# ScalarE's order in the second attention, step sizes in four blocks, and the first unit's waits by feature

## The reference

```python
def second_block(x, w_in, conv_w, conv_b, dt_bias, a_log, ...):
    proj = jnp.einsum('bsd,de->bse', x, w_in[layer])
    q, k, v, z_att, z_ssm, xbc, dt_raw = jnp.split(proj, list(SPLITS), axis=-1)
    # three dilated windows over q, k, v (dilations 1, 4, 16), 16 heads of 64,
    # put together by the softmax of their log-sums
    xbc = jax.nn.silu(causal_depthwise_conv(xbc, conv_w[layer], conv_b[layer]))
    dt = jax.nn.softplus(dt_raw + dt_bias)          # 16 numbers per token
    # chunked state-space scan over xbc and dt, norms, out projection, residual, layer norm
```

## Time and profile before

| | us |
|---|---|
| Median of 3 runs | 1773.06 (1771.41 to 1774.6) |
| The profiled execution | 1772.61 |
| Its span in the trace | 1770.8 |
| TensorE busy | 1717.6 (97%) |
| VectorE busy | 1187.0 (67%) |
| GpSimd busy | 888.1 (50%) |
| ScalarE busy | 812.8 (46%) |

### The profile page before, as it was taken

The page is one execution under the profiler, slowest core; times in us unless marked ns, Lnnn a source line. Parts: engine busy times, 40 slices in busy tenths (PEclk is TensorE's granted clock), DMA queues, the critical chain, the costliest instruction groups (busy, mean ns, idle before and its releaser), DMA issues.

```text
span 1770.8 us, 30057 instructions
## 1 busy us (share of the span) xinstructions
PE 1717.6 (97%) x11616; PEld 893.3 (50%) x11794; DVE 1187.0 (67%) x2237; ACT 812.8 (46%) x1622; POOL 888.1 (50%) x805
## 2 busy tenths in 40 slices
PE   8999999999999999999999999999999999999998
PEld 5534455455444456544445455544455555555543
DVE  5768889999999688431445578967155555555647
ACT  4523554443312677412322378843255655555720
POOL 0511543662661223687810257979566555772750
PEclk9999999999999999999999999999999999999999
DMA  9010111202321112212411246512211112111512
GB/s 399 26 54 36 54 48 66 78 24 102 161 96 52 68 66 102 120 59 105 180 60 70 93 165 197 199 35 98 89 39 53 58 34 58 34 52 56 207 65 95
DMA packets 53373, 161.84 MB, mean 91 GB/s; under 512 B 7056, under 2 KB 21776, under 8 KB 49008
## 3 DMA queue, kind: packets, MB, share of 16 engines
q1 hardware_dynamic: 49008, 136.36, 21.6%
q0 software_dynamic: 4224, 23.56, 3.4%
HBM read 129.35 MB, written 27.39 MB: 89 GB/s over the span
## 4 chain that ended last, share of the span: by engine, by line
PE 67%; DVE 20%; POOL 3%; ACT 3%; issue 3%; DMA 2%; SPq 0%; DVEq 0%; ACTq 0%; POOLq 0%
PE ps L1411 29%; PE ps L1891 14%; DVE small L2670 6%; PE ps L1405 4%; DVE arena L2423 4%; PE ps L1751 2%; PE ps L1434 2%; PE ps L1475 2%; PE ps L1533 2%; PE ps L1910 2%; DMA hT<-in_mods 2%; PE ps L1683 1%; PE ps L1507 1%; PE ps L1448 1%; PE ps L1515 1%
## 5 line engine op out<-in xcount | busy, mean ns | idle before, releaser
L1411 PE MATMUL ps<-hT,W 128*128 128x512 bf16 x2359 | 529.2, 381 | 10.5 <-ACT arena L1994 3.4
L1411 PEld LDWEIGHTS ps<-hT,W 128*128 128x128 bf16 x2424 | 236.1, 98 | 291.6 <-issue 12.2
L989 POOL TENSOR_TENSOR W<-W 128x512 bf16<-128x512 f32 x133 | 155.1, 1202 | 259.8 <-DMA W<-in_loads 189.6
L1411 PE MATMUL ps<-W,arena 128*128 128x512 bf16 x918 | 207.0, 380 | 1.1
L2097 ACT ACTIVATE arena<-arena,small 128x128 f32<-128x128 f32 (+9 forms) x192 | 123.1, 642 | 139.1 <-DVE small L2500 119.7
L1411 PEld LDWEIGHTS ps<-W,arena 128*128 128x128 bf16 x936 | 91.2, 97 | 112.0
L2670 DVE TENSOR_SCALAR_CACHE_REDUCE small<-arena,small 128x640 bf16<-128x640 f32 (+1 forms) x124 | 126.5, 1077 | 1.1
L974 POOL TENSOR_TENSOR arena<-arena 128x512 f32<-128x512 f32 (+1 forms) x62 | 104.8, 1691 | 43.6 <-DMA arena<-gates_scratch 19.1
L1411 PE MATMUL ps<-arena,W 128*128 128x512 bf16 x569 | 124.6, 379 | 1.2 <-POOL arena L1050 0.6
L2106 ACT ACTIVATE arena<-arena,small 128x128 f32<-128x128 f32 (+9 forms) x192 | 113.9, 644 | 18.6 <-DVE small L2458 18.6
L1891 PE MATMUL ps<-arena,W 128*128 128x512 bf16 x475 | 109.6, 379 | 1.1 <-issue 0.3
(11 more groups left out here) (391 smaller groups left out, 3225.8 us busy)
## 6 DMA issues: line engine op xcount, KB each, us to landing
W<-in_loads SPq DMA_DIRECT2D x20, 2048.0 KB, 8.0
arena<-sums_scratch SPq DMA_DIRECT2D x30, 512.0 KB, 4.6
W<-in_groups SPq DMA_DIRECT2D x56, 256.0 KB, 3.9
W<-in_loads SPq DMA_DIRECT2D x5, 1792.0 KB, 7.2
gates_scratch<-arena SPq DMA_DIRECT2D x32, 256.0 KB, 2.0
arena<-gates_scratch POOLq DMA_DIRECT2D x2, 4096.0 KB, 13.3
W<-in_mods SPq DMA_DIRECT2D x2, 2048.0 KB, 17.0
hT<-in_mods SPq DMA_DIRECT2D x2, 2048.0 KB, 21.3
```

The costliest lines, as they stand in the source:

```text
L989: last = nc.gpsimd.tensor_tensor(low(v), v, high(v), ALU.subtract)
L1411: last = mm(o, left[:, :, a], moving, start=(k == 0 and (a, b) == PRODUCTS[0]), stop=(k == steps - 1 and (a, b) == PRODUCTS[-1]))
```

## The change

Three edits. The `dt` units no longer run 512 tokens through 16 columns of the array: each product is four matmuls of 128 tokens, and each of the four writes its own strip of 32 partitions of PSUM. ScalarE puts them side by side with four copies. The wait for all 16 low parts ahead of the third unit of `xbc0` becomes one wait for each feature block inside that unit. In the second attention ScalarE's order within an iteration becomes: exponents of n, scalings of n, high parts of n-1, reads of sums. The first attention keeps its order.

```diff
-                if name == "dt":
-                    return KD, [(full, lambda k: parts(dt_weights[:, k, :]), lambda k: acts(hT, k, half, 512))]
...
+                if name == "dt":
+                    for k in range(KD):
+                        left = parts(dt_weights[:, k, :])
+                        for a, b in PRODUCTS:
+                            for r in range(4):
+                                last = mm(ps[32 * r:32 * r + 16, unit_bank(u), 0:P], left[:, :, a],
+                                          h_parts(k, 512 * i + P * r, P)[:, :, b], start=(k == 0 and (a, b) == PRODUCTS[0]),
+                                          stop=(k == KD - 1 and (a, b) == PRODUCTS[-1]), skip_group_check=True)
+                    last.then_inc(s_unit, 1)
+                    return
...
+                        if (name, i) == ("xbc0", 1):
+                            pe.wait_ge(s_hlow, KD + KD + k + 1)
...
-            pe.wait_ge(s_hlow, KD + 16)
...
+                elif name == "dt" and i < 2:
+                    for r in range(4):
+                        last = A(dtT[0:16, 512 * i + P * r:512 * i + P * r + P], ps[32 * r:32 * r + 16, unit_bank(u), 0:P],
+                                 ACT.Copy)
...
                         A(t, t, ACT.Exp, bias=mneg4[...], scale=-1.0, accum_out=den[...]).then_inc(sems["exp"], 1)
-                    extra(n, 0)
-                    if n >= 1:
-                        high_parts(n - 1)
+                    if tiles is at1:
+                        extra(n, 0)
                     act.wait_ge(sems["inverse"], n + 1)
                     act.wait_ge(sems["exp"], 2 * n + 2)
                     for x in range(2):
                         A(t, t, ACT.Copy, scale=rden[...]).then_inc(sems["scaled"], 1)
+                    if tiles is at2:
+                        if n >= 1:
+                            high_parts(n - 1)
+                        extra(n, 0)
                     extra(n, 1)
                     value_parts(n)
```

More of the change, by code:

```diff
@@ L1388, in unit @@
                     return
-                rows_ = slice(0, 72 if name == "small" and i < 2 else 16 if name == "dt" else P)
+                if name == "dt":
[8 more added lines that the diff above has]
+                    return
+                rows_ = slice(0, 72 if name == "small" and i < 2 else P)
                 steps, pieces = operands(name, i)
@@ L2006, in evac @@
                     last = A(gate[:, 512 * r:512 * r + 512], bank, ACT.Copy)
+                elif name == "dt" and i < 2:
+                    for r in range(4):
+                        last = A(dtT[0:16, 512 * i + P * r:512 * i + P * r + P], ps[32 * r:32 * r + 16, unit_bank(u), 0:P],
+                                 ACT.Copy)
                 elif name == "dt":
-                    last = A(dtT[0:16, half], bank[0:16], ACT.Copy) if i < 2 else A(dtr, bank[:, 0:128], ACT.Copy)
+                    last = A(dtr, bank[:, 0:128], ACT.Copy)
                 elif name == "sums":
```

## The result

The changed kernel takes 1779.2 us (median of 8 runs, 1776.58 to 1781.65) where the kernel before takes 1773.24 (8 runs, 1771.41 to 1776.69): a ratio of 1.0029, 95% interval 1.0018 to 1.0039. It is 6.0 us, 0.3%, slower; the forecast was 1780.2. Its profiled execution took 1777.69 us with a span of 1775.9.

A forecast was written before the change was run, and what follows sets the result against it. TensorE, busy 97% of the span, was taken to bound the kernel. 16.7 us lost less 9.6 gained, +7.1 on 1772.61, gave 1779.7, or 1780.2 on the median; range 1768 to 1788.

The forecast's parts named there:

- The sum: Whole kernel: 16.7 us lost (10.6 and 6.1), 9.6 gained (6.2, 1.9, 1.5), so 7.1 us slower.
- The strips: Step size (dt) units: 192 matmuls take 3.7 us, saving 6.5; four copies lose 0.35; net 6.2 gained, bounds 4.6 and 7.3.
- The rival in which strips take turns: dt units: strips don't run side by side, 10.2 us, edit saves nothing and costs 0.35; kernel 1786.7; chance 0.07.
- The waits by feature: Third unit of xbc0: no wait left after the last turn, 1.9 us gained, and 1.5 more from full clock.
- The 1.5 for the clock: Third unit of xbc0: without the standstill it runs at full clock, 1.5 us gained, bounds 0 and 1.5.
- The rival in which the clock falls all the same: Third unit of xbc0: clock falls anyway since turns with gaps stay ahead; 1.5 us more, 1781.7; chance 0.08.
- The pair ends: Second attention, six pair ends: TensorE waits 1.02 us each for the read of product 0, 6.1 us; bounds 0 and 8.
- the rival in which only the last pair pays: Pair ends: the read of product 0 is in time; 6.1 us less, 1774.1; chance 0.12.
- The last pair: Second attention's end: loop grows 12.9 us by scalings and 0.35 delays, less 2.3 slack: 10.6 lost; bounds 6 and 12.9.
- The order costs nothing: Pair ends and last pair: ScalarE's and VectorE's delay stays under TensorE's fillers, only gains count; 1763.5; chance 0.15.
- A fall in the longer waits of the last pair: Last pair: an aside that a clock fall there would cost about as much as one at the third unit, 1.5 us.

The follow-up runs named there:

- E1: The changed kernel with ScalarE's old order put back, so strips and waits by feature only: 1763.24 us, ratio 0.9949 to the kernel before.
- E2: The kernel before with only the new order of ScalarE's work: 1789.2 us, ratio 1.0094.
- E5: Strips and waits by feature, with ScalarE's new order only from item 56 on, the last pair: 1773.17 us, ratio 0.9999 to the kernel before.
- E6: Strips and waits by feature, with ScalarE's new order only for items 0 to 55: 1769.96 us, ratio 0.998 to the kernel before.
- E3: The kernel before with only the step sizes in four strips, the one wait for all low parts kept: 1766.3 us, ratio 0.9966.
- E8: E1 with the 192 step size matmuls all in one strip instead of four: 1770.64 us, 7.4 over E1.
- E4: The kernel before with only the waits by feature: 1769.78 us, ratio 0.9983.
- E7: E1 with the second attention's order exponents, reads of sums, scalings, high parts: 1774.53 us, 11.3 over E1.
- E10: E1 with the second attention's order exponents, high parts, scalings, reads of sums: 1762.39 us, 0.9 under E1.
- E9: E1 with the second attention's high parts of n-1 first waiting for the reciprocal of n, old order otherwise: 1763.38 us, 0.1 over E1.
- the base: The changed kernel with ScalarE's old order, that is strips and waits by feature only: 1763.24 us.
- E11: E1 with the step size units in two strips of two token blocks each instead of four strips: 1765.25 us, 2.0 over E1.

## Why the prediction was right, by its steps

- **The sum: right, in part by luck.** Forecast 16.7 lost and 9.6 gained, +7.1. Measured 16.0 lost (the changed kernel less E1; 15.5 if each is taken against the kernel before of its own group; 16.5 in E2, 16.6 in E5 and E6) and 9.5 gained (E1). The changed kernel is 6.0 over the kernel before. But the 16.7 were to be waits alone, and the waits are 13.8. The rest, 2 to 3 us, is the clock, for which the sum had no term: two terms too large and one at nothing made up for each other.
- **The strips: the term was mis-sized.** I took 19 ns from the narrow tiles of the earlier trace rows, between bounds of 13.3 and 27.5; it is 14, near the lower bound. The two units take 2.7 us and not 3.7. The copies took some of it back: four cost 1.11 and not 0.9 to 0.95. The kernel gained 6.4 (E3), against 6.2 net; in the trace the stretch of the two units and their copies is 7.1 shorter, and the difference is within what five runs can tell. The row that I leaned on holds 24 matmuls within 0.46 us including the step to the next line; over so short a stretch its edges count, and the bounds from quarter length and full overlap were the better guide. L1705 showed it already: its 0.0275 is a quarter of 0.11, and a full-width f32 transpose of as many columns takes 0.118, so four strips ran at once with no loss. For bf16 the same quarter of 0.053 was the value to expect. The rival in which strips take turns is E8, and falls: it would have cost 7.4. By the Trainium skill ("TensorE: Matmul & The Clock Gate", Wait — 56ns, not 53.3ns?) matmuls of 128 columns start every 55.8 ns at the upper level of the clock, and never closer than about 25 ns however few the columns. E8's 10.71 us over 192 are 55.8 ns each and agree; the floor of 25 doesn't hold across strips, where the trace of the changed kernel has 14.
- **The waits by feature: right in the wait, too firm on the clock.** The 1.9 us are gained in every trace without the old wait. The 1.5 for the clock I tied to the standstill, from two places of one execution. E3 kept the standstill and its execution had no fall there. By E4 about 1 us comes back on the mean of runs. The rival in which the clock falls all the same did not happen in any of the ten traces with the waits by feature, where the turns stay with their gaps and the unit has clock 1.00.
- **The pair ends: right in the mechanism, a fifth too large.** Forecast six waits of 1.02, 6.1 us. The lists of waits have 6.1 (E2), 6.2 (E6) and 4.8 (changed kernel), but from item 0 to item 56 each of the three is 5.1 to 5.2 longer, 0.83 at most pair ends, and by time it is 4.7 (the changed kernel less E7). VectorE's delay was sized at 1.33, and the exponents of item 48 come 1.17 later. E7 and E10 show the mechanism as it was put: the copy is late because it stands behind the high parts and these behind VectorE's delay; undo either and nothing waits. With that the rival in which only the last pair pays falls.
- **The last pair: right in the mechanism, too large in the waits.** Forecast 10.6 with item 55. By time it is 9.9 without item 55 (E5), which looks like a hit, but the waits in that are 4.7 and 2.8, which leaves 2.4 for the clock; with 1.2 for item 55 the waits are 8.7. The loop was to grow by 12.9 less 2.3 of slack; it grew by 4.2 less than 12.9. E9 shows the price of the scalings and of the wait apart. I had expected waits of 2 us at each odd item for L2479 (L2496 in the changed kernel); they are 1.5 at most, and VectorE's addition (L3151) and the turns take the rest.
- **The order costs nothing** was the rival on the other side. Its point of decision was a growth of 1.4 us per iteration against 2.3 us of slack over all nine. E9 is that rival come true at 0.35 per iteration: the slack took 2.3 of 3.15. At 1.35 it could not.
- **A part that I had only as an aside.** "A fall in the longer waits of the last pair would cost about as much": it is in the changed kernel's profile twice. Busy time and granted clock:

```profile
1651.00:1653.00 2.00, 1.96 (x7) 1.19 (x8) 1.93 (x6) 0.49 (x2) 1.17 (x1) 0.50 0.09 25
1696.00:1698.00 2.00, 2.00 (x6) 0.76 (x5) 0.00 (x0) 1.97 (x3) 0.00 (x0) 0.50 0.00 0
```

The first costs next to nothing, the second the 1.4 us behind the last pair. It isn't peculiar to this execution: the mean granted clock over all runs is 0.9958 in the changed kernel, 0.9956 in E7 and 0.9962 in E5, and 0.9975 to 0.9980 in every kernel on the base whose last pair has the old place of the high parts (E1, E6, E8 to E11). 0.0020, the changed kernel's less E1's, is 3.6 us of 1779, of which waits hide a part; the changed kernel itself takes 1776.6 us in the run at a clock of 0.998 and 1780.6 on the mean of the two at 0.994. My "10.6" had no term for it and still came out, since the loop grew by less than I counted: that is luck.

**What stays open.** E1 and E10 are both about 10 us faster than the kernel before and can't be told apart with five runs each. Of the order's 16 us the waits are 13.8 in the traces; what the clock takes differs from execution to execution (1.4 to 4.1 us in four), and its mean is known only as the rest, 2 to 3 us. Which part of the pair's loop hid the 1.9 us of growth that the prediction had counted and the trace doesn't have is not shown. Why the clock falls in one execution and not in another is not shown by any run.

## What to carry to other kernels

When an engine's queue is reordered, price what moves back, stage by stage: the scalings came 0.5 us (item 60) to 1.2 us (item 48) earlier, for which TensorE had waited 0.8 us in all, and the high parts came 1.35 us later (item 60) in a loop that passes them once per item, free mid pair under 5.1 us of fillers and about a us per item (8.7 over nine) where the fillers are 0.65 or 1.3. A delay costs only what is past the slack, so read the slack first (0.35 per item cost 0.8 us over nine items of the same loop). Count a cost from the starts of the same instruction in both traces: a list of waits also has gaps that were there before. And time the edits of a change one by one: two of these three are worth 9.5 us, and the third hid them.

## What the runs showed of the hardware

- Four column strips of 16 columns, with 128 x 16 bf16 weights and 128 moving columns, start a matmul every 14 ns; one strip every 56, two every 28. No floor shows down to 14.
- ScalarE copies 16 x 128 out of PSUM four times in 0.74 us when all lie on partitions 0 to 15 (E8), and in 1.09 to 1.11 when they lie on four groups of partitions (the changed kernel) or on two (E11) and go to partitions 0 to 15. The rows of E8, against those of the changed kernel:

```profile
914.40 0.74 ACT L2019 ACTIVATE small<-ps 16x128 f32<-16x128 f32 x4 [3.82 <-PE ps L1393]
...
919.76 0.74 ACT L2019 ACTIVATE small<-ps 16x128 f32<-16x128 f32 x4 [4.62 <-PE ps L1393]
```

- The falls of the clock, some 3 to 10 us each, come in some executions and not in others. The clearest place is one that no edit touches: from 336 to 342 us, behind two us in which TensorE does nothing, the granted clock is 0.63 to 0.82 in nine of the thirteen traces and 1.00 in four (the changed kernel, E3, E5, E7). One profile can't put a price on a fall at a given place; the mean clock over several runs can.
- A fall costs little where TensorE waits for others anyway: 0.1 us or less between items 56 and 63, against 1.4 for one as long right behind the last pair.
